# Plain float32 products of a prologue rewritten as three float32r products each

## The reference

```python
def token_mixer(h, w_in, b_in, ...):
    p = h @ w_in + b_in
    y_a = hyena_branch(p[..., :ML_START], ...)                       # three 512-wide parts, short conv, long conv
    y_b, state = mlstm_branch(p[..., ML_START:GATE_START], ...)      # q, k, v, o, gates; 4 heads
    g_a, g_b = jnp.split(jax.nn.sigmoid(p[..., MERGE_START:]), 2, axis=-1)
    return (g_a * (y_a @ w_branch_hy) + g_b * (y_b @ w_branch_ml)) @ w_out, state
...
        ada_x = jnp.split(s_lat @ w_ada[l] + b_ada[l], 6, axis=-1)
        ada_c = jnp.split(s_ctx @ w_ada[l] + b_ada[l], 6, axis=-1)
        hc = modulate(rmsnorm(ctx, norm_mix_g[l]), ada_c[0], ada_c[1])   # 256 context tokens
        hx = modulate(rmsnorm(x, norm_mix_g[l]), ada_x[0], ada_x[1])
        yx, _ = token_mixer(hx, *mix_params, rows, GRID_W, ctx_state)
        x = x + ada_x[2][:, None, :] * yx
        hx2 = modulate(rmsnorm(x, norm_ffn_g[l]), ada_x[3], ada_x[4])
        x = x + ada_x[5][:, None, :] * expert_choice_ffn(hx2, w_router[l], w_exp1[l], w_exp3[l], w_exp2[l])
```

## Time and profile before

| | |
|---|---|
| median of 3 runs | 2394.13 us (2393.95 to 2395.83) |
| profiled execution, time / span | 2395.29 us / 2393.5 us |
| PE products, weight loads | 2017.4 us (84%), 1349.3 us (56%) |
| DVE, ACT | 926.1 us (39%), 605.5 us (25%) |
| DMA | 660.68 MB, mean 276 GB/s |
| prologue | to the first expert's weights at 402.86 us |

### The profile page before, as it was taken

One profiled execution on the slowest core, in us unless ns is written; L12 is line 12 of the kernel. 1 busy time (PEld: TensorE's weight loads), 2 busy tenths in 40 slices (PEclk: granted clock), 3 DMA queues, 4 the chain that ended last, 5 costly groups with the idle time before them and its releaser, 6 DMA issues. The chain is left out here.

```text
span 2393.5 us, 26012 instructions
## 1 busy us (share of the span) xinstructions
PE 2017.4 (84%) x11114; PEld 1349.3 (56%) x11114; DVE 926.1 (39%) x1213; ACT 605.5 (25%) x698; POOL 0.2 (0%) x4
## 2 busy tenths in 40 slices
PE   7999997666666666776666799999999999989998
PEld 3586664222222222222222688887888888888887
DVE  5423423000000000000000767566767676557766
ACT  3311201000000000000000434463434434554333
POOL 0000000000000000000000000000000000000000
PEclk9999997888888888778788899999999999999999
DMA  9148164999999999999999445434554645434552
GB/s 396 71 159 331 73 251 192 430 435 431 430 432 434 430 430 433 433 431 429 434 431 428 177 177 185 184 124 150 197 199 176 221 179 184 180 139 145 195 189 97
DMA packets 34085, 660.68 MB, mean 276 GB/s; under 512 B 3784, under 2 KB 4296, under 8 KB 6224
## 3 DMA queue, kind: packets, MB, share of 16 engines
q1 hardware_dynamic: 31984, 651.60, 66.9%
q10 hardware_dynamic: 2016, 7.84, 0.9%
HBM read 658.38 MB, written 1.05 MB: 276 GB/s over the span
## 5 line engine op out<-in xcount | busy, mean ns | idle before, releaser
L1341 PE MATMUL ps<-u_both,w_hi 128*128 128x512 f32 (+1 forms) x1792 | 545.2, 364 | 0.0
L1106 DVE TENSOR_TENSOR ring_lo<-ring,w_hi 128x2048 fp32r<-128x2048 f32 x168 | 384.8, 2291 | 224.2 <-ACT w_hi L579 224.1
L1341 PE MATMUL ps<-u_both,ring_lo 128*128 128x256 f32 x1536 | 430.7, 280 | 0.0
L579 ACT CAST w_hi<-ring 128x2048 fp32r<-128x2048 f32 x168 | 320.0, 1905 | 226.2 <-PE ps L1341 224.8
L1341 PEld LDWEIGHTS ps<-u_both,w_hi 128*128 128x128 f32 x1792 | 319.7, 188 | 58.5 <-issue 0.7
L1341 PEld LDWEIGHTS ps<-u_both,ring_lo 128*128 128x128 f32 x1536 | 290.1, 189 | 1.6
L1341 PE MATMUL ps<-ring,area_h 128*32 128x512 f32 (+1 forms) x1088 | 185.2, 767 | 71.5 <-DMA ring<-experts_dram 63.7
L1341 PE MATMUL ps<-ring_b,area_h 128*32 128x512 f32 x1024 | 161.3, 793 | 81.3 <-DMA ring_b<-experts_dram 72.8
L1096 DVE TENSOR_TENSOR expert_area<-expert_area,ps 128x512 f32<-128x512 f32 x16 | 11.0, 688 | 452.7 <-PE ps L1341 452.7
L558 ACT COPY expert_area<-ps 128x1024 f32<-128x1024 f32 x16 | 16.2, 1012 | 615.5 <-PE ps L1341 615.5
L1341 PEld LDWEIGHTS ps<-ring,area_h 128*32 128x32 f32 (+1 forms) x1088 | 49.3, 141 | 200.2 <-issue 113.7
(11 more groups left out here) (308 smaller groups left out, 2066.5 us busy)
## 6 DMA issues: line engine op xcount, KB each, us to landing
ring<-stream_dram SPq DMA_DIRECT2D x116, 2048.0 KB, 7.8
ring_b<-experts_dram SPq DMA_DIRECT2D x48, 4096.0 KB, 31.1
ring<-experts_dram SPq DMA_DIRECT2D x48, 4096.0 KB, 31.0
area_n<-norm_rows_dram ACTq DMA_DIRECT2D x6, 512.0 KB, 4.2
tail<-filt_out_dram SPq DMA_DIRECT2D x1, 1536.0 KB, 6.4
tables<-tabs_dram ACTq DMA_DIRECT2D x1, 1408.0 KB, 13.4
tabs<-tabs_dram ACTq DMA_DIRECT2D x1, 1296.0 KB, 10.5
x_tok<-x_dram SPq DMA_DIRECT2D x1, 1024.0 KB, 8.9
```

Source lines behind the costliest of these rows:

```text
L579: A.copy(upper_part(n), ring[:, n % RING, :]).then_inc(sig("alone_hi_ready") if n in ALONE else sig("w_hi_ready"), 1)
L1106: V.tensor_tensor(ring_lo[:, n % RING, :], ring[:, n % RING, :], upper_part(n).bitcast(F32), ALU.subtract).then_inc(sig("alone_ready") if ...
L1341: ins = M.matmul(out, lhsT, rhs, start=start, stop=stop, **more)
```

## The change

All products with weight slots of the prologue but those of the modulation rows become three float32r products. For that 30 slots are split; the upper parts go to three places in turn (the space of x, which is reloaded later, and two places of the ring; late ones to `area_h`), so the ring has six slots behind the first eight. ACT's casts (`upper_first`) and DVE's subtractions (`lower_first`) stand between the evacuations and convolutions; GpSimd makes the first two lower parts. The input is split too: ACT writes the upper part of x and context, DVE writes the same value unrounded and subtracts. k units on x start with one block of the width at a time, in four banks. q moves behind v, beside Hyena's parts; the second modulation row goes between these units, one slot after each two; o goes into the state loop; more merge gates into the heads, as plain sums whose sigmoid follows later; the third modulation row goes between the merge gates of the second order. The branches' mLSTM half goes before the Hyena half, and the merged result is split on DVE. Quads 2 and 3 of the experts wait until all 54 slots are used.

```diff
+FIRST_RING = 6
+ADA_SLOTS = (tuple(range(8)), tuple(range(13, 29, 2)), (36, 37, 39, 40, 41, 43, 44, 45))
+FIRST_SPLIT = (8, 9, 10, 11) + tuple(range(12, 28, 2)) + tuple(range(28, 36)) + (38, 42) + tuple(range(46, FIRST_SLOTS))
+HEAD_UNITS = ((25, 26), (27,), (28, 29), (30,))
...
+        def first_upper(i):
+            if i % 3:
+                return ring_lo[:, FIRST_RING - 1 + i % 3, :]
+            return x_r[:, :] if i < 24 else area_hr[:, SLOT:]
...
+            for i in range((FIRST_SLOTS - RING) // 2):
+                sp.wait_ge(sig("slot_used"), 2 * i + (2 if i < 3 else 4))
+                if 2 * i + 4 == FIRST_SPLIT[21] + 2:
+                    sp.dma_start(x_tok[:, :, :], d["x"]).then_inc(sig("x_loaded"), 16)
+                load(i % 3, PAIRS + i)
...
+            def upper_first(i):
+                n = FIRST_SPLIT[i]
+                act.wait_ge(sig(f"pair_loaded{first_place(n) // 2}"), first_turn(n) * 16 + 16)
...
+                    act.wait_ge(sig("slot_used"), FIRST_SPLIT[i - 3] + 1)
+                A.copy(first_upper(i), ring[:, first_place(n), :]).then_inc(sig("first_hi"), 1)
...
+            for i in range(8):
+                for c in (4 + 2 * i, 5 + 2 * i):
+                    to_conv(c, col("b_q", c - 4) if c < 8 else col("b_hy", c - 8), T)
+                upper_first(6 + i)
...
+            def lower_first(i):
+                dve.wait_ge(sig("first_hi"), i + 1)
+                at = first_place(FIRST_SPLIT[i])
+                V.tensor_tensor(ring_lo[:, at, :], ring[:, at, :], first_upper(i).bitcast(F32),
+                                ALU.subtract).then_inc(sig("first_lo"), 1)
...
+        @block.gpsimd
+        def _(pool):
+            for i in range(2):
+                pool.wait_ge(sig("first_hi"), i + 1)
+                at = first_place(FIRST_SPLIT[i])
+                nc.gpsimd.tensor_tensor(ring_lo[:, at, :], ring[:, at, :], first_upper(i).bitcast(F32),
+                                        ALU.subtract).then_inc(sig("first_lo_p"), 1)
...
+            pe.wait_ge(sig("hT_lo"), 1)
+            pe.wait_ge(sig("first_hi"), 2)
             for k in range(KD):
+                pe.wait_ge(sig("hT_hi"), 1 + k + 1)
+                for u in range(4):
+                    for p in range(2 if u == 0 else 1):
+                        mm(bank(u)[:, 0:T], first_four(u, p, k), xT[0][:, k, :], start=k == p == 0, stop=False)
+                if 1 <= k <= 4:
+                    pe.wait_ge(sig("hT_tmp"), k)
+                    turned_in(k + 3)
+            pe.wait_ge(sig("first_lo_p"), 2)
...
+            def unit(b, i, j):
+                w = split_first(i)
+                for k in range(KD):
+                    a = j * 1024 + k * P
+                    last = k == KD - 1
+                    product3(b[:, 0:T], [v[:, a:a + P] for v in w], [v[:, k, :] for v in xT], k == 0, last,
+                             free=int(last and j == 1), ready=sig("unit_ready") if last else None)
...
+            for i in range(8):
+                for j in range(2):
+                    unit(unit_bank(5 + 2 * i + j), 4 + i, j)
+                if i == 0:
+                    pe.wait_ge(sig("v_kept"), 1)
+                ada(4, range(i, i + 1), 1)
...
-                    merge_units(38, 39)
+                    merge_units(37, 38)
+                    ada(7, range(2, 4), 2)
+                    merge_units(39)
+                    ada(7, range(4, 5), 2)
+                    merge_units(40)
+                    ada(7, range(5, KD), 2)
```

More of the change, by code:

```diff
@@ new lines, in _ @@
+            upper_first(0)
+            upper_first(1)
+            act.wait_ge(sig("mod1_ready"), 1)
+            for k in range(KD):
+                act.wait_ge(sig("hT_ps"), k + 1)
+                for i, out in enumerate((xT[0], cT[0])):
+                    last = A.activation(out[:, k, :], bank(4 + (k + 1) % 4)[:, i * T:(i + 1) * T], ACT.Identity,
+                                        scale=mod1[:, i, k:k + 1], bias=ada_cols[:, i, k:k + 1])
+                last.then_inc(sig("hT_hi"), 1)
@@ L433, in _ @@
+            upper_first(2)
             act.dma_start(vbias[:, :], d["vbias"]).then_inc(sig("biases_loaded"), 16)
             act.dma_start(wrouter[:, :, :], d["wrouter"]).then_inc(sig("biases_loaded"), 16)
+            act.dma_start(tables[:, :], d["tabs"]).then_inc(sig("tabs_loaded"), 16)
             act.dma_start(fin_rows[:, :], d["fin_rows"][0]).then_inc(sig("fin_loaded"), 16)
[L436 to L442, removed]
@@ L1444, in _ @@
-            b = unit_bank(0)
-            for k in range(KD):
-                pe.wait_ge(sig("hT_ready" if k % 2 else "hT_ready_a"), k // 2 + 1)
-                mm(b, wg_wide[:, k, :, :].rearrange("p g h -> p (g h)"), hT[:, k, :], start=k == 0, stop=k == KD - 1,
-                   ready=sig("unit_ready") if k == KD - 1 else None)
-            def features(units, at, width):
-                for i, n in enumerate(units):
-                    w = slot(at + i // 2)
-                    b = unit_bank(n)
-                    for k in range(KD):
-                        a = (i % 2) * 1024 + k * P
-                        mm(b[:, 0:width], w[:, a:a + P], hT[:, k, 0:width], start=k == 0, stop=k == KD - 1,
-                           free=int(k == KD - 1 and i % 2 == 1), ready=sig("unit_ready") if k == KD - 1 else None)
@@ new lines, in _, with with_context @@
+            pe.wait_ge(sig("first_lo_p"), 2)
+            for k in range(KD):
+                pe.wait_ge(sig("hT_lo"), 1 + k + 1)
+                for u in range(4):
+                    mm(bank(u)[:, 0:T], first_four(u, 0, k), xT[1][:, k, :], start=False,
+                       stop=u == 0 and k == KD - 1)
+                    if u > 0:
+                        mm(bank(u)[:, 0:T], first_four(u, 1, k), xT[0][:, k, :], start=False, stop=k == KD - 1)
+            def with_context(u, b):
+                for k in range(KD):
+                    if u == 0:
+                        pe.wait_ge(sig("hT_lo"), 1 + KD + k + 1)
+                    last = k == KD - 1
+                    product3(b[:, T:], [first_four(u, p, k) for p in range(2)], [v[:, k, :] for v in cT],
+                             k == 0, last, free=int(last and u % 2 == 0 and u > 0),
+                             ready=sig("unit_ready") if last else None)
@@ new lines, in branch @@
+            def branch(k, g):
+                pe.wait_ge(sig("hT_lo"), 1 + 2 * KD + 2 - g)
+                w = split_first(22 + k // 2)
+                if k >= 4 and g == 1:
+                    pe.wait_ge(sig("gated"), k - 3)
+                for i in range(4):
+                    a = (k % 2) * 1024 + g * 512 + i * P
+                    last = g == 0 and i == 3
+                    product3(bank(k % 4)[:, g * T:(g + 1) * T], [v[:, a:a + P] for v in w],
+                             [v[:, 4 * g + i, :] for v in y_r], i == 0, i == 3,
+                             free=int(last and k % 2 == 1), ready=sig("branch_ps") if last else None)
@@ L1637, in _ @@
+            for k in range(4):
+                branch(k, 1)
+            ada_turn(2, 7)
+            for k in range(4):
+                branch(k, 0)
+            for k in range(4, KD):
+                branch(k, 1)
+                branch(k, 0)
             for g in range(2):
```

475 lines of the change are left out of this document (267 added, 208 removed).

## The result

| | median us (runs) | lowest to highest |
|---|---|---|
| before | 2394.98 (4) | 2393.95 to 2396.58 |
| after | 2363.65 (4) | 2362.12 to 2372.03 |

The ratio is 0.9873 (95% interval 0.9861 to 0.9885): 31 us less. The profiled executions took 2395.29 and 2362.65 us, 32.6 less. Four more runs of the same changed kernel, timed later, had a median of 2367.89 (0.9886, interval 0.9871 to 0.9901); the experiments come back to that difference.

The account below looks back on a forecast made before the run. TensorE was taken to bound the prologue, DMA the expert phase. 44.1 - 2.5 - 3.0 - 0 - 1.6 = 37.0, less 1.9 for cross-engine waits, gave 35.1 us off 2395.29: median 2359 us, range 2350 to 2377.

Parts of the forecast that it names:

- milestone of 331 us: End of the prologue's output product, which the prediction expected near 331 us in the new profile.
- Term 1: TensorE's products throughout the prologue: three float32r products in place of plain float32 take 44.1 us less.
- Term 2: First units at the start: TensorE waits for upper and lower parts of the turned input, loss 2.5 us.
- Term 3: Weight splits: landing, cast and subtraction take 12.0 us, hidden in the q and Hyena loop; loss 3.0 at its end.
- Term 4: The four heads, with six units put in: 37.0 us in all, 2.8 more than before, called no loss.
- Term 5: Hyena orders to the output product: DVE late for second order and branch halves, net loss 1.6 us; merging about level.
- Experts: Expert weight quads 2 and 3 load after all 54 slots, arriving 12 us early: cost nothing.
- (a): Rival: prologue waits are smaller than summed, at best all 44.1 us gained, 2350 us; chance 0.12.
- (b): Rival: split chain late, with merging and GpSimd a loss of up to 12 us, 2364 to 2377; chance 0.22.
- (d): Rival: split chain governs all of some 27 splits, slower than before, 2416 us at 13 us landing; chance 0.05.
- (e): Rival: float32r products in the prologue are no faster than plain ones, 2394 us; chance 0.02.
- (c): Rival: a wait drops TensorE's clock to 1.2 GHz, granted below 1 before the routing; 3 to 5 us, 2364; chance 0.04.

Follow-up runs that it names:

- the control: The changed kernel itself timed again with no edit, beside three other kernels on the same chip: median 2367.89 us, ratio 0.9886.
- fillers: Changed kernel plus eleven unread identity matmuls in TensorE's idle time at the start (41.2 to 46.2 us): median 2364.37 us.
- the experiment: Changed kernel with the upper-weight, lower-input product left out in the 16 q and Hyena loop units, two of three products remaining: median 2360.36 us.
- the three edits: Changed kernel with second start cast on DVE, last Hyena output's upper half before split 24's cast, split 13 behind the weighted keys: median 2357.78 us, ratio 0.9848.

## Why the prediction came out as it did

The direction was right, and so was the mechanism of the gain; one wait and one clock loss at the start were not seen. The end was 4.7 us low by the first four runs and 9 by those of the control. Up to the output product the gain was 7.5 us smaller than the prediction's milestone of 331 us has it, and the routing returned 3.1 because the clock fell later in this profile than before. That was luck: in the control's profile the routing took 36.95 us, 1.1 more than before. By its steps:

- **Term 1** (44.1). Of the right size: about 42. v takes 22.2 us (79.5 to 101.7) and the output product 22.1, as forecast; the one k unit that is made in one piece is evacuated 5.69 us after the unit before it, for 5.65. The 256-token unit is 2.88, since its triples come every 0.36 us and not 0.353 as in the earlier trace rows: 36 x 0.58 = 20.9 in place of 22.7. The Trainium skill (FP8 and Floating Point Precision, TensorE Precision Notes) has true FP32 in four passes, by which a plain unit would cost a third more; the loop with plain products says the same as the rows: 3.46 against 2.88, a fifth more.
- **Term 2** (loss 2.5). The step that failed. It has GpSimd's subtraction with the words "the first can start at about 36.5 us", which puts the cast ahead of it at about 34.6, and gives no landing for the weights. They are requested at 26.60 and land at 41.4, behind the backlog of the start. The trace before has the same load at 18.4 us from its issue at 26.24. With that, two casts of 1.9 stand before the evacuations, the start is at 46.20 and not about 43, and PE's 5 us of idle let the clock fall, another 1.5 or so (fillers). With units at 5.65 from 43.79 the v products would begin at 72.0; they began at 79.5. Loss 7.5, which is 5.0 more than forecast. GpSimd, which I had watched, was free: no wait of PE is released by it. The Trainium skill gives 4497 ns for such an operation (GPSIMD Engine Reference, 3.1); the trace agrees with 4.53 and 4.58 us.
- **Term 3** (loss 3.0). The chain was about right: at most 12.3 against 12.0 by the experiment, no wait in eight rounds. The wait for the first state weights was 1.70 for 1.8, the state copies 0.56 for 1.2. Missed was the round itself, 6.94 for 6.62, 2.5 us in all: 0.22 at each modulation step between units (1.8 in all), the rest in the triples, which term 1 above has already. The 1.9 that I had set aside for cross-engine waits (18 at 0.1 are 1.8) is as large, but it was meant for something else.
- **Term 4** (0). 213.73 - 177.16 = 36.6 us for 37.0.
- **Term 5** (1.6). The 1.97 at the last output was 1.3 in the forecast, and the 1.50 at unit 39 was called hidden: I had counted DVE's lateness for the spectrum products, which have cover, and not PE's for the lower part itself, whose slot is requested late. Together about 2 more. The merging did not bind: PE has no wait for a lower part in the output product. It has one of 1.07 us for the normalisation of the first result (`area_n`, at 336.23), which the longer products had covered before.
- **Experts.** Cost nothing, but with less cover than said: the third and fourth load are issued at 339.60 and DMA is through at about 365 us, 6 us ahead of the first expert, not 12. The loads took 25 us where the prediction counted 24, and of the 35.9 us that it had for cover 31.7 were there.
- **Rivals.** (a), (b), (d) and (e) did not happen: no wait of PE in the loop is released by a lower part. (c) did, beside the forecast: I had bounded it by my waits, which were under 3 us. The first was 5 us, and it brought the clock to 0.83 in 40 to 60 us, so the sign that the prediction named for (c) was there. Its chance of 0.04 hung on the size of the waits, and that was the term that was wrong. The Trainium skill describes idle gaps between products that throttle the array again and again (TensorE: Matmul & The Clock Gate, HAM oscillation); the wait at the start agrees: without fillers there, the granted clock of 40 to 60 us is 0.83 in every profile but that of the three edits, where the wait is 2.2 us and the clock 0.91. The later waits of 1.5 to 3 us did so in some executions and not in others; what decides between them no run here settles. In (b), the stated terms give 2359 + 12 = 2371; the 2377 of the range has no term for the other 6.

## What to carry to other kernels

When a producer is put in front of a stage, look up when its input lands, not only when its engine is free: one late slot moved the start of this kernel by 3 us, and the trace before already showed that load behind a backlog. In a chain of small waits an edit that removes one shows in the milestones and can be lost again behind them; three edits that gave nothing measurable alone gave 5.0 us together at the first expert, and 6 or 10 in the median, by which of the two sets of runs of the changed kernel it is held against. And PE's idle time has two prices, the wait and the clock behind it: a wait that cannot be shortened can be filled with products that nobody reads. Time a kernel again before a difference of a few microseconds is laid to an edit: here the same program moved its median by 4.2 us.

## What the runs showed of the hardware

- The same program varied between 2362 and 2372 us in eight executions, before the change between 2393 and 2397. The two profiles of it put the difference at stretches behind waits of 1.6 to 2.1 us, where PE's granted clock stands at 1.00 in one and falls in the other (1.00 and 0.66 in 295 to 300 us, 1.00 and 0.85 in 340 to 350). That shorter waits or fillers lessen the scatter is not shown: it was 2.5 us with three waits shortened and 2.5 in the control, and 7.2, 7.0 and 4.2 us in the kernels with fillers in the routing.
- Matmuls of the identity in the waits of the routing kept the clock at 1.00 from 340 to 360 us and nearly halved the time of what follows (7.03 to 3.75 us for 32 gathering products). Without those ahead of the zero products it fell at 345 us in one profile all the same (0.62 in 340 to 350).
- A modulation step of 8 narrow products costs 1.18 us between units, and 0.96 where two stand together (1.92).
- GpSimd's subtraction of 128 x 2048 took 4.53 and 4.58 us, twice DVE's 2.29, and did not slow DVE's evacuations of PSUM beside it (0.46 us each with and without).
